# Filler matmuls of ones on TensorE at the start of a streaming encoder step and behind the sums between its stages

## What is computed

```python
h = rms_norm(x, norm_w[layer, 0])
m = mixer(h)                                  # HGRN2 or latent attention
x = x + rms_norm(m, norm_w[layer, 1])
f, buf = conv_ffn(rms_norm(x, norm_w[layer, 2]), ...)
x = x + rms_norm(f, norm_w[layer, 3])
```

## Time and profile before

| | |
|---|---|
| median of 3 runs | 2703.89 us (2703.53 to 2704.15) |
| the profiled execution | 2704.65 us |
| its span in the profile | 2702.7 us |
| TensorE busy | 2652.8 us, 98% of the span |
| VectorE, ScalarE, GpSimd busy | 65%, 48%, 15% |
| mean granted clock of TensorE | 0.993 |

### The profile page before, as it was taken

One profiled execution on the slowest core, in us unless ns is written; L12 is line 12 of the kernel. 1 busy time (PEld: TensorE's weight loads), 2 busy tenths in 40 slices (PEclk: granted clock), 3 DMA queues, 4 the chain that ended last, 5 costly groups with the idle time before them and its releaser, 6 DMA issues.

```text
span 2702.7 us, 55248 instructions
## 1 busy us (share of the span) xinstructions
PE 2652.8 (98%) x19742; PEld 2636.6 (98%) x19742; DVE 1759.1 (65%) x2892; ACT 1300.6 (48%) x2173; POOL 412.0 (15%) x792
## 2 busy tenths in 40 slices
PE   8999999999999999999999999999999999999997
PEld 8999999998999999999999999999999999999997
DVE  7787878847766634676644855548766535666644
ACT  6556566545444433444444566545444433444443
POOL 1111111100322100222200000001322101222200
PEclk9999999999999999999999999999999999999999
DMA  6444444443554555544455422344554555545553
GB/s 224 134 150 138 137 141 138 131 155 127 177 165 163 161 166 164 168 162 167 153 173 167 148 90 81 118 160 133 171 166 161 163 164 166 170 158 169 159 168 116
DMA packets 122671, 413.57 MB, mean 153 GB/s; under 512 B 13856, under 2 KB 20160, under 8 KB 122592
## 3 DMA queue, kind: packets, MB, share of 16 engines
q1 hardware_dynamic: 114480, 406.37, 46.8%
q10 hardware_dynamic: 7056, 3.21, 0.4%
q0 software_dynamic: 1056, 2.92, 0.3%
HBM read 406.97 MB, written 5.48 MB: 153 GB/s over the span
## 4 chain that ended last, share of the span: by engine, by line
PE 94%; DVE 4%; ACT 1%; issue 1%; DMA 0%; POOL 0%; SPq 0%; DVEq 0%; ACTq 0%
PE bank L229 30%; PE bank L231 29%; PE bank L230 29%; DVE w_lo L223 1%; DVE X L1112 1%; DVE Y L1109 1%; PE bank L793 1%; PE bank L1654 1%; DVE h_lo L1096 1%; PE bank L752 1%; PE bank L794 0%; ACT w_hi L216 0%; PE bank L759 0%; DVE Y L1126 0%; PE bank L1659 0%
## 5 line engine op out<-in xcount | busy, mean ns | idle before, releaser
L229 PE MATMUL bank<-h_hi,w_hi 128*128 128x288 f32 (+1 forms) x4208 | 1269.7, 302 | 28.2 <-DVE h_lo L1096 12.4
L223 DVE TENSOR_TENSOR w_lo<-raw,w_hi 128x1024 fp32r<-128x1024 f32 (+2 forms) x786 | 955.9, 1226 | 468.2 <-ACT w_hi L216 467.2
L230 PE MATMUL bank<-h_lo,w_hi 128*128 128x288 f32 (+1 forms) x4208 | 1253.5, 298 | 0.0
L231 PE MATMUL bank<-h_hi,w_lo 128*128 128x288 f32 (+1 forms) x4208 | 1250.0, 297 | 0.0
L216 ACT ACTIVATE w_hi<-raw 128x1024 fp32r<-128x1024 f32 (+2 forms) x786 | 808.0, 1037 | 864.0 <-PE bank L231 854.4
L229 PEld LDWEIGHTS bank<-h_hi,w_hi 128*128 128x128 f32 x4208 | 793.8, 189 | 34.6 <-issue 26.7
L231 PEld LDWEIGHTS bank<-h_hi,w_lo 128*128 128x128 f32 x4208 | 796.9, 189 | 0.2
L230 PEld LDWEIGHTS bank<-h_lo,w_hi 128*128 128x128 f32 x4208 | 795.5, 189 | 0.7
L1272 POOL TENSOR_TENSOR ext<-yt,small 128x256 f32<-128x256 f32 x176 | 212.2, 1206 | 1511.5 <-ACT yt L1167 1033.9
L229 PE MATMUL bank<-g_hi,w_hi 128*128 128x288 f32 x1408 | 416.8, 296 | 0.0
L230 PE MATMUL bank<-g_lo,w_hi 128*128 128x288 f32 x1408 | 415.5, 295 | 0.0
(11 more groups left out here) (250 smaller groups left out, 2051.2 us busy)
## 6 DMA issues: line engine op xcount, KB each, us to landing
raw<-in_w_fi SPq DMA_DIRECT2D x352, 512.0 KB, 3.9
raw<-in_w_hi_in SPq DMA_DIRECT2D x128, 512.0 KB, 4.1
raw<-in_w_fo SPq DMA_DIRECT2D x128, 512.0 KB, 3.6
raw<-in_w_fo SPq DMA_DIRECT2D x64, 384.0 KB, 3.5
raw<-in_w_ho SPq DMA_DIRECT2D x32, 512.0 KB, 4.1
raw<-in_w_mo SPq DMA_DIRECT2D x32, 512.0 KB, 3.8
raw<-in_w_down SPq DMA_DIRECT2D x18, 512.0 KB, 4.4
raw<-in_w_ukv SPq DMA_DIRECT2D x16, 512.0 KB, 3.7
```

The lines of the kernel that those rows point to most:

```text
L223: dve.tensor_tensor(w_lo[:, ch.slot, 0:n], raw[:, ch.slot, 0:n], w_hi[:, ch.slot, 0:n].bitcast(F32), ALU.subtract).then_inc(lo_done, 1)
L229: pe.matmul(out, w_hi[:, ch.slot, w], rhs_hi, start=start, stop=False)
L230: pe.matmul(out, w_hi[:, ch.slot, w], rhs_lo, start=False, stop=False)
L231: return pe.matmul(out, w_lo[:, ch.slot, w], rhs_hi, start=False, stop=stop)
```

## The change

TensorE gets a helper, `keep_busy`, that issues n matmuls of 128 moving columns: ones with ones, read as float32r, into psum[7]. None of them waits for anything but what stood before on TensorE, and none raises a semaphore. It is called with 115 at the begin, between the wait for `filled` and the first products, and with 55 at the end of `norm_pe` in stages 1, 2 and 3.

```diff
@@ norm_pe
             pe.matmul(psum[4][:, 0:T], ones[:], ssq[:], start=True, stop=False)
             pe.wait_ge(y_squared, KT * s)
             pe.matmul(psum[4][:, 0:T], ones[:], sq[:], start=False, stop=True).then_inc(n_sum, 1)
+            if stages[s][1]:
+                keep_busy(pe, 55)
+
+        def keep_busy(pe, n):
+
+            for _ in range(n):
+                pe.matmul(psum[7][:, 0:P], ones[:].bitcast(F32R), ones[:].bitcast(F32R), start=True, stop=True)
@@ block.tensor
             pe.wait_ge(filled, 1)
+            keep_busy(pe, 115)
             run_hgrn(pe, hgrn_pe, lambda e: (gemm_first(e, IN, 0), ...
```

## The result

| | before | with the change |
|---|---|---|
| median | 2703.89 us (2703.37 to 2704.15, 5 runs) | 2718.30 us (2717.81 to 2718.55, 5 runs) |
| ratio | | 1.0053, 95% interval 1.0043 to 1.0064 |
| span of the profiled execution | 2702.7 us | 2716.4 us |
| TensorE busy in it | 2652.8 us | 2685.8 us |

What follows compares the result with a forecast made beforehand. TensorE, busy 98% of the span, was taken as the bound, with gains only where it waits or runs slowly. Begin +2.7 us and handoffs 0 on the 2703.89 median gave 2706.6 us, range 2701.8 to 2728.

Steps and rivals of the forecast that it cites:

- the likeliest case: Whole kernel: begin costs +2.7 us, handoffs 0, giving 2706.6 us, within 0.2% of no change; chance 0.40.
- rival 2: Begin and handoffs: fillers don't count as work for the clock; +13.8 us and some 8, sum +22, 2726 us; chance 0.27.
- the prediction's own sign: Begin: prediction wrong if L1009 moves by other than the fillers' overrun less 2.6 us.
- If they bring the clock up after the same 5.9 us as the products did: Begin: fillers raise TensorE's clock after 5.9 us, as the first products did, whatever the slow work consists of.
- The term of the sum built on it: Begin: 28 fillers at 0.21 us, 87 at 0.112, last ends at 16.7; whole program behind moves by +2.7 us.
- the 2.6 us of the products behind the fillers: Begin: first 25 products take 5.9 us instead of 3.3; with the clock up, 2.6 us comes back.
- What a filler costs: Begin and handoffs: the weight load sets a filler's pace, 0.112 us at full clock and 0.21 at half.
- The path behind the begin: Behind the begin: chunk 4's split, squares and L1009 follow TensorE's later sum, so the whole program moves +2.7 us.
- The handoffs at 0: Three handoffs: fillers cost 0, covered by VectorE's pace to row 6 of h; gain at most 0.09 us, in stage 3.
- the limit of 635.3: First handoff: TensorE could start as late as 635.3 us and still reach row 6; only what passes that costs.
- Rival 1: Begin: cheap fillers, 0.06 to 0.08 us, end before h's first row; -1.8 us, handoffs at most 0.1, 2702.0; chance 0.20.
- Rival 3: Begin and handoffs: narrow float32r matmul costs 0.22 us like plain float32; +15 and 13, sum +28, 2732 us; chance 0.10.

Runs made afterwards that it cites:

- the wide filler: 38 fillers of 384 columns at the begin, none in the handoffs, against the kernel before the change: 2702.68 us, ratio 0.9995.

## Why the prediction was right in part

**The range held, the likeliest case didn't.** 2718.3 lies within 2701.8 to 2728, and slower by over 0.2% had 0.38; the forecast was 2706.6 and no measurable change. The kernel did rival 2's begin and the forecast's handoffs. That the range held is luck in part: it reached to 2728 for the sake of rival 2, whose 8 us in the handoffs didn't come, and no case on record gave the time that was measured. By the prediction's own sign it was wrong: L1009 was to move by the overrun less 2.6 us, and it moved by 14.28 less 0.5.

**The step that failed** is "If they bring the clock up after the same 5.9 us as the products did". They didn't in 24.6 us. The term of the sum built on it, 28 slow and 87 fast fillers, was +2.7 and measured +13.74. The same step gave back the 2.6 us of the products behind the fillers; 0.5 came back. The reading behind it was that a stretch of slow work counts whatever it consists of. No row of before could bear that out, since every slow stretch there was of wide products. The Trainium skill, TensorE: Matmul & The Clock Gate, section What's actually happening, says that the gate opens after a stretch of time and not after a number of matmuls. The prediction took the rows as agreeing; the 24.6 us of fillers here don't bear it out for this stream. The run with plain float32 fillers shows that the kind of matmul decides: records 0.213 us apart as well, and the clock was up after 5.6 us. What in the kind of matmul it is stays open.

**What a filler costs** was right: 0.112 taken for full clock, 0.110 to 0.115 measured in the handoffs; 0.21 for half clock, 0.2133 measured. The rows with 32 columns against whole weights were the ones to price it by. The Trainium skill, TensorE: Matmul & The Clock Gate, section Back-to-back issue gap, gives 81 ns for 128 columns. These float32r matmuls took 0.110 to 0.115 us, and the measurement decides.

**The path behind the begin** was right in every step: the split of chunk 4, the squares and L1009 moved with the sum behind chunk 6, by 13.73 or 13.74 us, and all behind them with it.

**The handoffs at 0** were right, with their reason: row 6 sets the pace up to there. The limit was right as well: with 100 fillers the cost was 8.4 us where the limit of 635.3 gives about 9.

**Rival 2** had its begin right (+13.8 against +13.74) and its handoffs wrong (+8 against 0). That the begin fits to 0.1 us is chance: the fillers took 0.5 us longer than its 0.21 each gives, and five slow products fewer gave 0.5 back. I had taken "the fillers don't count" as one statement on both places. At the begin they had to raise a clock that was down, in the handoffs to hold one that was up, and these proved to be different. Had the two been kept apart, the case that came true would have had a name and a time of its own, 2717.7. **Rival 1** was wrong of this filler, but its chain of consequences (sum 2.6 us early, L1009 held at 35.4 by the Exp, -1.8 us) is what the wide filler then did: 2.67, 35.24 and -1.8. **Rival 3** is out: a narrow float32r matmul took 0.213 at half clock and not 0.43, and 0.115 at full clock and not 0.22.

## What to carry to other kernels

A filler on an in-order engine is free only until the first real work is ready: count it at the slow clock's price, and end it before that moment (here 45 fit and 115 were issued). Look first at what a faster engine would wait for: in the handoffs VectorE's rows and squares set the pace, so a clock kept up was worth nothing, and at the begin 2.0 of 2.7 us came through. Try the filler's shape at the state in which it has to work, since one that holds the clock up need not raise it.

## What the runs showed of the hardware

- At the start of the program the clock is down. Narrow float32r matmuls (128 columns, 128x128 weights, 0.2133 us from start to start) left it down for 24.6 us in two traces. The same ones with 384 columns (0.32 us) raised it after 5.7, 4.9 and 3.2 us in three traces, plain float32 ones of 128 columns (0.213 us for a record) after 5.6 us in one, products of 288 columns after 3.9 to 6.0 us in four.
- The same narrow stream held the granted clock at 1.00 for 6.3 and for 11.3 us in the handoffs, where the kernel before, without it, fell to 0.5.
- Narrow float32r matmuls with 128x128 weights of ones start 0.110 to 0.115 us apart at full clock and 0.213 at half. Plain float32 records of only 32 columns hold the engine for 0.112 us as well, so the weight load, and not the columns, is the likely limit. Under 288 columns it is hidden (0.133 from start to start).
- The record of the granted clock is silent before its first change and reads 1.00 there, while starts 0.24 us apart show the lower level.
